# A two-layer RWKV-7 and retention decoder step: values centred ahead of the retention products, branch A's last sums on GpSimd, and other opening orders in the feed-forward and in the second layer

## The reference

```python
h = _rmsnorm(x, p['norm_mix_pre']);  z = h @ p['w_in']
ya, s_wkv, s_shift = _rwkv7_branch(za, ...)            # 8 heads of 64, delta rule with decay
yb, s_ret = _retention_branch(zb, pos, s_ret, gn_g, gn_b)
m = sigmoid(ga) * (ya @ p['w_out_a']) + sigmoid(gb) * (yb @ p['w_out_b'])
x = x + _rmsnorm(m @ p['w_o'], p['norm_mix_post'])
h = _rmsnorm(x, p['norm_ffn_pre'])
f = (silu(h @ p['w_ffn_gate']) * (h @ p['w_ffn_up'])) @ p['w_ffn_down']
x = x + _rmsnorm(f, p['norm_ffn_post'])
# in the retention branch, for each of 8 heads (key width 64, value width 128):
inner = (q k^T * d_in) @ v;  cross = (q @ S) * d_q;  o = inner + cross
S = S * d_c + (k * d_k)^T @ v
yb = ((o - mean(o)) * rsqrt(var(o) + eps) * gain + bias) * silu(gate)   # mean, var over the 128 values of a head
```

## Time and profile before

| | |
|---|---|
| median of three runs | 1308.31 us |
| the profiled execution | 1308.13 us, of which the span is 1306.4 us |
| TensorE matmul busy | 1243.1 us, 95% of the span |
| VectorE, ScalarE, GpSimd busy | 862.6, 551.2, 128.4 us |
| granted TensorE clock, mean | 0.984 |

### The profile page before, as it was taken

One profiled execution on the slowest core, in us unless ns is written; L12 is line 12 of the kernel. 1 busy time (PEld: TensorE's weight loads), 2 busy tenths in 40 slices (PEclk: granted clock), 3 DMA queues, 4 the chain that ended last, 5 costly groups with the idle time before them and its releaser, 6 DMA issues.

```text
span 1306.4 us, 27689 instructions
## 1 busy us (share of the span) xinstructions
PE 1243.1 (95%) x11984; PEld 1167.4 (89%) x11984; DVE 862.6 (66%) x1440; ACT 551.2 (42%) x841; POOL 128.4 (10%) x144
## 2 busy tenths in 40 slices
PE   6999999999998999999899998999999989999996
PEld 5899887898997999999798987888899979999996
DVE  4887568877766665653477954688777657566433
ACT  5553434443445433343444533344444454333432
POOL 0004473000000000000000071900000000000000
PEclk9999999999998999999999999999999989999998
DMA  6433235544353644544433323355444534444441
GB/s 225 129 116 115 66 104 177 196 146 146 127 168 101 189 146 149 157 146 147 144 97 113 125 75 86 95 181 181 145 147 134 160 101 145 147 154 146 151 149 69
DMA packets 51176, 179.50 MB, mean 137 GB/s; under 512 B 6256, under 2 KB 7024, under 8 KB 49776
## 3 DMA queue, kind: packets, MB, share of 16 engines
q1 hardware_dynamic: 42576, 153.77, 37.7%
q10 hardware_dynamic: 8480, 23.97, 5.2%
HBM read 166.57 MB, written 8.53 MB: 134 GB/s over the span
## 4 chain that ended last, share of the span: by engine, by line
PE 81%; DVE 8%; ACT 3%; POOL 3%; DMA 2%; issue 2%; ACTq 0%; SPq 0%; DVEq 0%; POOLq 0%
PE dense L1310 50%; PE core L1310 31%; DVE w_lo L857 2%; ACT w_hi L564 1%; DMA wkv_s<-s_st 1%; DVE x L905 1%; POOL qk_rot L521 1%; DVE y_out L903 1%; POOL rot_tmp L519 1%; POOL qk_rot L518 1%; DMA qk_rot<-qk_raw 1%; DMA x<-x_t 0%; POOL s_st L532 0%; DVE bonus L968 0%; DVE y_a L1164 0%
## 5 line engine op out<-in xcount | busy, mean ns | idle before, releaser
L857 DVE TENSOR_TENSOR w_lo<-w_raw,w_hi 128x1024 fp32r<-128x1024 f32 x282 | 350.9, 1245 | 237.3 <-ACT w_hi L564 236.8
L564 ACT ACTIVATE w_hi<-w_raw 128x1024 fp32r<-128x1024 f32 x282 | 298.0, 1057 | 474.8 <-PE dense L1310 317.3
L1310 PE MATMUL dense<-h_hi,w_hi 128*128 128x320 f32 x1296 | 418.4, 323 | 28.7 <-DVE h_lo L861 14.6
L1310 PE MATMUL dense<-h_hi,w_lo 128*128 128x320 f32 x1296 | 404.9, 312 | 0.0
L1310 PE MATMUL dense<-h_lo,w_hi 128*128 128x320 f32 x1296 | 404.8, 312 | 0.0
L1310 PEld LDWEIGHTS dense<-h_hi,w_hi 128*128 128x128 f32 x1296 | 247.0, 191 | 45.0 <-issue 33.5
L1310 PEld LDWEIGHTS dense<-h_lo,w_hi 128*128 128x128 f32 x1296 | 247.6, 191 | 4.3 <-issue 2.4
L1310 PEld LDWEIGHTS dense<-h_hi,w_lo 128*128 128x128 f32 x1296 | 247.3, 191 | 0.0
L1310 PE MATMUL core<-h_hi,w_hi 128*128 128x320 f32 x416 | 129.5, 311 | 0.0
L1310 PE MATMUL core<-h_lo,w_hi 128*128 128x320 f32 x416 | 129.0, 310 | 0.0
L1310 PE MATMUL core<-h_hi,w_lo 128*128 128x320 f32 x416 | 129.0, 310 | 0.0
(11 more groups left out here) (295 smaller groups left out, 1987.9 us busy)
## 6 DMA issues: line engine op xcount, KB each, us to landing
w_raw<-wts SPq DMA_DIRECT2D x282, 512.0 KB, 3.5
ret_t<-ret_t ACTq DMA_DIRECT2D x16, 256.0 KB, 3.7
ret_s<-ret_t ACTq DMA_DIRECT2D x16, 256.0 KB, 2.4
ret_rest<-ret_d ACTq DMA_DIRECT2D x2, 1536.0 KB, 6.6
qk_rot<-qk_raw SPq DMA_DIRECT2D x8, 320.0 KB, 6.2
dmask<-rconst ACTq DMA_DIRECT2D x2, 1152.0 KB, 5.6
s_st<-wkv_st ACTq DMA_DIRECT2D x2, 1024.0 KB, 5.0
wkv_s<-s_st ACTq DMA_DIRECT2D x2, 1024.0 KB, 8.1
```

What stands on the lines that cost most here:

```text
L564: act.activation(w_hi[n % RING][:, :], w_raw[n % RING][:, :], ACT.Copy).then_inc(hi_ready.sem, 1)
L857: dve.tensor_tensor(w_lo[r][:, :], w_raw[r][:, :], w_hi[r][:, :].bitcast(F32), ALU.subtract).then_inc(low_made.sem, 1)
L1310: return pe.matmul(out, lhsT, rhs, start=start, stop=stop)
```

## The change

1. **Centred values.** The mean over a head's 128 outputs is linear in the values, so each value row has its own mean taken off before mixing. VectorE sums `v_tok` (`sum_values`, two reductions and a small scaling), GpSimd adds the negative mean into `v_cent` (two buffers), and `cross` gets the same from `cross_sum`. The mean products on TensorE and lines 1241 and 1242 on VectorE go; ScalarE squares `o_b` (one 640-wide operation, `squared_b`).
2. **State update in four pieces.** `kexp` holds 4 sequences instead of 8 in each half, and the update products are four of 32 rows by 256 columns instead of two of 64 rows by 512, into `core[0], core[1], core[3], core[4]`. VectorE's `ret_t` update is four operations of 256.
3. **Branch A's finish.** GpSimd multiplies by the root and adds the bonus (640 wide, in two halves); VectorE only splits.
4. **Norms.** `acc` sums seven squares; TensorE adds the eighth itself with a second product; ScalarE takes the root ahead of the next `w_hi`; VectorE's `w_lo` of the eighth block moves behind the third group of `x`, whose `h_lo` both come at once.
5. **Openings.** The feed-forward's first four tiles go input block by input block. The second layer's opening follows a written order, and its fourth tile's `w_hi` and `w_lo` move ahead of the root.
6. `finish_yb` of the last pass moves behind the second output block of `T_WOA`.

```diff
+OPEN_NEXT = [(k, i) for k in range(4) for i in range(2)] + [(k, 2) for k in range(4)] + [(k, 0) for k in range(4, 8)] \
+    + [("sum", 0), ("sum", 1), (4, 1), (5, 1), (6, 1), ("pick", 0), (7, 1)] + [(k, 2) for k in range(4, 8)]
 @block.gpsimd, behind rotate(7)
+                for hp in range(HP):
+                    pool.wait_ge(*v_summed(layer, hp + 1))
+                    if hp == 0:
+                        pool.wait_ge(*seq_done(layer, SEQ_AT["s3", SAMPLE]))
+                    elif hp >= 2:
+                        pool.wait_ge(*mixed(layer, hp - 1))
+                    pool.tensor_tensor(v_cent[hp % 2][:, 0:512]..., v_pair(hp), bc(sums[:, 0:4]...), ALU.add)
+                    pool.tensor_tensor(v_cent[hp % 2][:, 512:640]..., v_sample(hp)..., ALU.add).then_inc(v_centred.sem, 1)
+                    if hp == 0:
+                        finish_ya(0)
+                        finish_ya(1)
 @block.scalar, x_root, gates, project_out
+                    if k == 1 and layer:
+                        high(RING)
-                    gates(nxt, nxt + sum(FILL))
+                    gates(nxt, nxt + FILL[0])
+                    act.wait_ge(*mixed_evac(layer, hp + 1))
+                    act.activation(sq_b[...], o_b[...], ACT.Square).then_inc(squared_b.sem, 1)
+                    gates(nxt + FILL[0], nxt + sum(FILL))
-                        high(after(c))
+                        if c < KT - 1:
+                            high(after(c))
+                    norm_root(k)
+                    high(after(KT - 1))
 @block.vector, norm_add and the passes
-                        if c:
+                        if 0 < c < KT - 1:
-                            while done < lo:
+                            while done < (hi if i == 2 else lo):
                                 after(done)
                                 done += 1
+                            if i == 2:
+                                for n in lows(KT - 1):
+                                    low(*n)
-                    link(dve.tensor_copy(cross[:, :], core[2][:, 384:512]))
+                    link(dve.tensor_reduce(cross_sum[:, :], core[2][:, 384:512], AX.X, ALU.add))
+                    link(dve.tensor_scalar(cross_sum[:, :], cross_sum[:, :], -1.0 / 128, None, ALU.mult))
+                    link(dve.tensor_scalar(cross[:, :], core[2][:, 384:512], cross_sum[:, 0:1], None, ALU.add))
+                        sum_values(hp + 1)
-                    link(dve.tensor_tensor(y, y, ch(sq_a, i), ALU.mult))
-                    link(dve.tensor_tensor(y, y, ch(bonus, i), ALU.add))
+                    dve.wait_ge(*ya_sum(layer, i // 2 + 1))
 @block.tensor
+                    mm(core[0][:, 0:T], ones, acc[:, :], True, False)
+                    pe.wait_ge(*y_squared(layer, k * KT))
+                    mm(core[0][:, 0:T], ones, ch(sq8, KT - 1), False, True).then_inc(sum_done.sem, 1)
+                    pe.wait_ge(*v_centred(layer, hp + 1))
-                    for par in range(2):
-                        own = slice(C * par, C * par + C)
-                        ins = mm(core[par][:, :], v_sample(hp)[own], kexp[own, :])
+                    for q in range(2):
+                        for par in range(2):
+                            own = slice(C * par + 32 * q, C * par + 32 * q + 32)
+                            ins = mm((core[par], core[3 + par])[q][:, 0:256], v_sample(hp)[own], kexp[own, :])
-                    for par in range(2):
-                        mm(core[3 + par][:, 0:T], ones, ch(o_b, 2 * hp + par)).then_inc(mean_b.sem, 1)
+                    both = [(one, k) for one in (0, 2, 1, 3) for k in (k0, k0 + 1)]
+                    if ready:
+                        both.sort(key=lambda u: u[1])
```

More of the change, by code:

```diff
@@ L809, in _, with project_out @@
                 high(T_WO + 2 - 1)
-                def project_out(before, after, group0, gain):
+                def project_out(before, after, group0, gain, k):
                     for c in range(8):
@@ L1223, in _ @@
                         make_qexp(hp + 1)
+                        if hp:
+                            dve.wait_ge(*v_centred(layer, hp))
+                        sum_values(hp + 1)
                     if hp == 0:
@@ L1367, in x_pick, with opening @@
                     mm(core[0][:, 0:T], pick, acc[:, :]).then_inc(x_summed.sem, 1)
-                def opening(j0, g0, ready, first, between={}):
-                    for step in range(KT + 2 * RING - 2):
-                        if step in between:
-                            between[step]()
-                        for i in range(RING):
-                            k, j, g = step - 2 * i, j0 + i, g0 + i
-                            if not 0 <= k < KT:
-                                continue
-                            if k == 0:
-                                pe.wait_ge(*low_ready(layer, j))
-                                open_bank(g)
-                            if i == 0:
-                                pe.wait_ge(*ready(layer, first + k + 1))
-                            for n, (w, which) in enumerate(parts(j, k)):
-                                ins = mm(bank(g)[:, 0:T], w, ch((h_hi, h_lo)[which], k), k == 0 and n == 0, k == KT - 1 and n == 2)
-                            if k == KT - 1:
-                                ins.then_inc(tile_used.sem, 1)
-                def sums():
-                    x_sum(1, 0)
-                    x_sum(1, 1)
-                at = SUMS_AT[layer > 0]
-                opening(0, 0, h_ready, 0, {at: sums, at + 1: lambda: x_pick(1)})
+                def opening(j0, g0, ready, first, order):
+                    for k, i in order:
+                        j, g = j0 + i, g0 + i
+                        if k == "sum":
+                            x_sum(1, i)
+                            continue
+                        if k == "pick":
+                            x_pick(1)
+                            continue
+                        if k == 0:
+                            pe.wait_ge(*low_ready(layer, j))
+                            open_bank(g)
+                        if i == 0:
+                            pe.wait_ge(*ready(layer, first + k + 1))
+                        for n, (w, which) in enumerate(parts(j, k)):
+                            ins = mm(bank(g)[:, 0:T], w, ch((h_hi, h_lo)[which], k), k == 0 and n == 0, k == KT - 1 and n == 2)
+                        if k == KT - 1:
+                            ins.then_inc(tile_used.sem, 1)
+                opening(0, 0, h_ready, 0, OPEN_NEXT if layer else OPEN_FIRST)
                 pe.wait_ge(*lora_loaded(layer, 1))
@@ L1723, in _ @@
                                      for k in range(4)], ya_hi, ya_lo)
-                opening(T_WOB, G_WOB, yb_ready, 0)
+                opening(T_WOB, G_WOB, yb_ready, 0, [u for u in OPEN_FIRST if u[0] not in ('sum', 'pick')])
                 for c in range(RING, 8):
```

117 lines of the change are left out of this document (72 added, 45 removed).

## The result

Over five runs of each, interleaved, the changed kernel took 1297.39 us in the median (1293.04 to 1297.91), the kernel before 1308.31 (1304.92 to 1309.54). The ratio is 0.9915, with a 95% interval of 0.9893 to 0.9936. That is 10.9 us faster; I had forecast 22.8, and the time lies outside the range. The profiled execution took 1297.91 us against 1308.13.

A forecast was written before the change was run, and what follows sets the result against it. TensorE, busy 95% of the span, was taken as the bound. Savings of 13.8 (retention), 0.6 (T_WOA), 4.4 (mid-layer), 3.1 (into layer 1) and 0.5 (last norm) made 22.4 us: 1285.5 for the median, range 1279.5 to 1293.

The forecast's parts named there:

- The first passes: First retention pass of each layer: VectorE's chain is the bound and gets shorter, saving 1.5 us per layer, 3.0 together.
- Two or three of them plus a few splits fall into that time: 1.1 us: First passes: w_lo operations and splits on VectorE lose 1.1 us beside GpSimd's work (bounds 0 and 3).
- The second passes: Second retention passes: 1.67 us saved on TensorE in each, plus 0.75 us from a better clock in layer 1.
- TensorE's own 1.67 only lengthens its wait: First passes: the 1.67 us TensorE saves gain nothing there, since it waits for VectorE's chain anyway.
- the rival for slower: Pass heads: each of eight waits 2.2 us more for ret_t and brings the lower clock; 1315 us, chance 0.03.
- The third and fourth passes: Later passes of each layer: TensorE saves 1.67 us in each, 1.19 from the means and 0.48 from the strips.
- The slack of 0.3 us: End of the later passes: VectorE's last update and TensorE's products end within 0.3 us; no wait was costed.
- Openings and norms: Norms and the openings behind them: mid-layer 4.4 us, into layer 1 3.1 us, the last norm 0.5 us saved.
- The norm's term: Four norms: TensorE adds the eighth square itself, so the sum ends 0.53 us earlier at each.
- My half microsecond of clock per opening: Three openings: the half-clock stretch gets one microsecond shorter, saving 0.5 us at each (bounds -0.8 and 2.5).
- T_WOA: T_WOA's output blocks: a wait of 1.0 us replaces one of 1.28, saving 0.3 us per layer, 0.6 together.
- VectorE becomes the bound of the passes: Retention passes: first ones gain nothing, each other one waits 0.8 us for VectorE; 1293.5 us, chance 0.15.

The follow-up runs named there:

- nofinish: The changed kernel with GpSimd's four 640-column operations of branch A's finish cut to 16 columns each, leaving that output unfinished; 1291.29 us.
- late: The changed kernel with the second half of branch A's finish put off into the second pass, its splits on VectorE there; 1288.25 us.
- warm_after: The changed kernel with 24 unread TensorE products behind the norm's sum at each of three norms, and nothing else; 1288.57 us.
- late_roots: late with ScalarE's roots of the pass before moved ahead of the wait for the ret_t stores and the ret_t loads; 1288.59 us.
- norms_yb: The changed kernel with the norm's sum wholly on VectorE, branch B's last finish ahead of T_WOA and h_lo in the old places; 1302.23 us.
- warm: late_roots with 24 unread TensorE products of 320 columns behind the norm's sum at each of three norms; 1278.74 us.

## Why the prediction was wrong

- *The first passes* (forecast -3.0, measured +1.3). The step that failed is "Two or three of them plus a few splits fall into that time: 1.1 us". The two `w_lo` lost 2.6 us, `ya_lo` 0.72 and `ya_hi` 0.20 beside `v_cent`: 3.5 us where I had 1.1. I had priced a `w_lo` beside GpSimd from the earlier trace rows, where it met operations of other lengths at other phases. `nofinish` gives the price by itself. The other terms held: sums 1.1, updates 0.4, eight operations 4.2. One was missing from my sum: the wait for the third `w_hi`, 0.7 us (0.5 more than before in layer 0). Together the chain grew by 1.3 us in layer 0 and 1.5 in layer 1, where I had it 1.6 shorter. The rule that I cited against this part (the Trainium skill, SBUF - State Buffer, the port pair of VectorE and GpSimd: whoever starts first holds it for the whole instruction) is what the traces show for `w_lo`, with both operands in SBUF, to about 0.1 us. That layer 1's chain still ends 26.7 us behind the pass's start, as before (26.8), is luck: the wait of its first `w_hi` for a store was 1.6 us shorter. TensorE's own 1.5 us went into its wait.
- *The second passes* (forecast -4.1, measured -0.1). The step is "TensorE's own 1.67 only lengthens its wait". A wait is not free when it grows: it went from 2.0 to 3.5 us in layer 1 and from 0.7 to 3.5 in layer 0, and brought the lower clock into the next pass. `late` (no wait, clock 1.00) and `warm_after` (wait, 0.89) show both sides. I had this mechanism in the rival for slower, but only for a wait that I did not expect, not for the one that I had counted as harmless.
- *The third and fourth passes* (forecast -6.7, measured -6.0). Right in kind; 1.50 us each instead of 1.67, since the strips take 0.64 and not 0.58 us and the means had cost 1.08 and not 1.19. That no wait comes at their heads was right for a reason I had not seen: the wait at the first head gave ScalarE time for the stores. With that wait gone (`late`) TensorE waited 0.4 to 1.1 us there, and `late_roots` left 0.4 us at one head of each layer. The slack of 0.3 us that I had counted for VectorE ran through ScalarE and a DMA, which I had not followed.
- *Openings and norms* (forecast -8.0 with the end, measured -8.3). The norm's term was right (0.50 of 0.53, `norms_yb`). The sum came out right with its other parts spread otherwise. The window of the earlier trace rows around layer 0's opening had a clock of 0.57 and has 0.86, so the half clock there shrank from 10.2 to 3.4 us and not by one microsecond as I had it. The eight traces with the new openings, the new norm and no filling have 241.2 to 242.6 us for layer 0's feed-forward and 116.4 to 116.8 for layer 1's opening and projections. Against the one trace before that is 2.1 to 3.5 us where I had 2.2, and 1.9 to 2.2 where I had 2.6. My half microsecond of clock per opening is not measured by itself; taking away all the half clock that is left (`warm` against `late_roots`) gives 0.3 to 0.9 us per opening.
- *T_WOA* (forecast -0.6): right by `norms_yb`, 0.34 per layer, though the one profiled execution shows 0 (0.27 gained in layer 0, 0.26 lost in layer 1).
- *What I left at nothing*: the recurrence. It took 2.7 us more in the profiled execution after, in code that did not change. The traces of one and the same code there differ by over 6 us in layer 1, so scatter could make it. It is not shown to be that alone: nine of the ten later traces without filling have more than the 101.9 us of before, of which there is one trace.

Of the rivals, "VectorE becomes the bound of the passes" (1293.5) named the right engine. Its 4.8 us of waits in the later passes did not come; the first passes grew instead, and the clock fell behind them.

## What to carry to other kernels

Work moved to GpSimd beside VectorE is worth what VectorE's SBUF-only operations do not lose to it. Lay the GpSimd operations against VectorE's list by start and end, and put them where VectorE reads PSUM or waits; here moving half of them one pass later gave 9 us, and the offload itself 1 us per first pass.

Where TensorE waits, a saving ahead of the wait lengthens it, and a longer wait has a second price in the clock behind it. If the wait can't be closed, products that nobody reads can hold the clock (9.9 us between the medians here; the traces show 2.0 right behind the filled waits and 3.8 in the next layer's recurrence), at no cost to what waits.

Edits of 2 to 3 us are smaller than what the falls of the clock move from one execution to the next; compare the two traces stretch by stretch, and leave out the stretches that the edit can't touch.

## What the runs showed of the hardware that I had not expected

- VectorE and GpSimd take turns on operations that read and write SBUF alone, whole operation by whole operation, and both lose: `w_lo` 1.22 to 2.50 us, GpSimd's 640-wide addition 1.58 to 2.40, a cast of 320 columns 0.32 to 0.98. VectorE's `st<-core`, with an operand in PSUM, lost nothing (0.42 us).
- Four products in 32-row strips of 256 columns run together: 0.64 us for what two 64-row ones of 512 do in 1.06.
- TensorE kept 2.4 GHz through three norms on products of an idle operand into an unread bank, and through layer 1's recurrence in all four traces with this filling; all eleven without it fell to 1.2 GHz there. In layer 0's recurrence, ahead of the filling, six of those eleven kept 2.4 GHz as well.
